# Ring depths of a weight pipeline: three raw buffers, four high and four low parts

## What is computed

```python
proj = rms_norm(h, norm1_gain) @ w_in            # 2048 x 2048 and more
q = (xt @ w_q)                                   # peer_w_q
a = einsum('cd,ced->ce', xc, expert_u[ic])       # peer_u: 2048 x 16384
w = gc * gelu(a)
y = einsum('ce,ced->cd', w, expert_v[ic])        # peer_v: 16384 x 2048
u = square(relu(h @ w_up)); x = x + rms_norm(u @ w_down)
```

## Time and profile before

| | before |
|---|---|
| median of 3 runs | 3338.53 us (3335.76 to 3339.82) |
| profiled execution | 3337.88 us, span 3335.7 us |
| mean granted TensorE clock | 0.989 |
| TensorE busy | 3250.5 us, 97% |
| VectorE busy | 2020.4 us, 61% |
| ScalarE busy | 1490.8 us, 45% |
| DMA of the SyncE queue | 598.71 MB, 57.6% of 16 engines |
| low parts L1981 | 1101 times, mean 1223 ns |
| high parts L1760 | 1101 times, mean 1058 ns |

### The profile page before, as it was taken

One profiled execution on the slowest core, in us unless ns is written; L12 is line 12 of the kernel. 1 busy time (PEld: TensorE's weight loads), 2 busy tenths in 40 slices (PEclk: granted clock), 3 DMA queues, 4 the chain that ended last, 5 costly groups with the idle time before them and its releaser, 6 DMA issues.

```text
span 3335.7 us, 38691 instructions
## 1 busy us (share of the span) xinstructions
PE 3250.5 (97%) x15278; PEld 2704.2 (81%) x15278; DVE 2020.4 (61%) x2922; ACT 1490.8 (45%) x1876; POOL 539.9 (16%) x321
## 2 busy tenths in 40 slices
PE   8888999999999999999999999999999999999998
PEld 7677898788888888888888888888888788888886
DVE  6755568884444456666666665565465655555556
ACT  5434444444444444444444444445444544444443
POOL 0100004787778700000000000000000000000000
PEclk9889999999999999999999999999999999999999
DMA  6553456888888877777776665555666566666664
GB/s 207 179 206 95 145 174 189 200 206 207 209 213 205 208 275 247 244 246 245 241 243 217 183 198 183 158 176 172 189 189 199 176 188 189 189 189 189 189 189 151
DMA packets 215092, 658.71 MB, mean 197 GB/s; under 512 B 56128, under 2 KB 56272, under 8 KB 212352
## 3 DMA queue, kind: packets, MB, share of 16 engines
q1 hardware_dynamic: 165680, 598.71, 57.6%
q0 software_dynamic: 49232, 57.54, 7.7%
HBM read 620.38 MB, written 35.78 MB: 197 GB/s over the span
## 4 chain that ended last, share of the span: by engine, by line
PE 88%; DVE 8%; ACT 3%; issue 1%; DMA 0%; DVEq 0%; ACTq 0%; SPq 0%
PE bank L1554 86%; PE bank L1616 2%; DVE wlo L1981 2%; ACT whi L1760 1%; ACT M L1802 1%; DVE AL L2027 0%; DVE M L2267 0%; DVE M L2273 0%; DVE R L2459 0%; ACT M L1750 0%; DVE M L2271 0%; DVE M L2269 0%; DVE M L2084 0%; DVE TMP L2050 0%; DVE M L2284 0%
## 5 line engine op out<-in xcount | busy, mean ns | idle before, releaser
L1981 DVE TENSOR_TENSOR wlo<-raw,whi 128x1024 fp32r<-128x1024 f32 x1101 | 1343.8, 1223 | 1082.1 <-ACT whi L1760 1077.7
L1760 ACT ACTIVATE whi<-raw 128x1024 fp32r<-128x1024 f32 x1101 | 1159.8, 1058 | 1301.5 <-PE bank L1554 1265.0
L1554 PE MATMUL bank<-whi,BH 128*128 128x512 f32 x2344 | 932.5, 398 | 12.8 <-DVE wlo L1981 7.7
L1554 PE MATMUL bank<-whi,BL 128*128 128x512 f32 x2344 | 915.3, 390 | 0.0
L1554 PE MATMUL bank<-wlo,BH 128*128 128x512 f32 x2344 | 913.8, 390 | 0.0
L1554 PE MATMUL bank<-whi,AH 128*128 128x512 f32 (+1 forms) x1952 | 772.4, 396 | 22.5 <-DVE AL L2027 15.2
L1554 PE MATMUL bank<-whi,AL 128*128 128x512 f32 (+1 forms) x1952 | 762.6, 391 | 0.0
L1554 PE MATMUL bank<-wlo,AH 128*128 128x512 f32 (+1 forms) x1952 | 762.0, 390 | 0.0
L2524 POOL DMA_INDIRECT scr_g<-M x256 | 495.0, 1934 | 437.3 <-issue 396.5
L1554 PEld LDWEIGHTS bank<-whi,BH 128*128 128x128 f32 x2344 | 440.9, 188 | 106.2 <-DVE wlo L1981 12.4
L1554 PEld LDWEIGHTS bank<-whi,BL 128*128 128x128 f32 x2344 | 440.5, 188 | 94.3
(11 more groups left out here) (240 smaller groups left out, 1600.6 us busy)
## 6 DMA issues: line engine op xcount, KB each, us to landing
raw<-in_peer_u SPq DMA_DIRECT2D x256, 512.0 KB
raw<-in_peer_v SPq DMA_DIRECT2D x256, 512.0 KB
raw<-in_w_in SPq DMA_DIRECT2D x160, 512.0 KB
raw<-in_w_up SPq DMA_DIRECT2D x128, 512.0 KB
raw<-in_w_down SPq DMA_DIRECT2D x128, 512.0 KB
raw<-in_w_out SPq DMA_DIRECT2D x64, 512.0 KB
raw<-in_w_in_a SPq DMA_DIRECT2D x32, 512.0 KB
scr_g<-M POOLq DMA_DIRECT2D x8, 2048.0 KB, 29.8
```

The lines of the kernel that those rows point to most:

```text
L1554: return e.matmul(outp, l, r, start=start, stop=stop)
L1760: e.activation(whi[:, n % NH, :], raw[:, n % NR, :], ACT.Copy).then_inc(s_hi, 1)
L1981: e.tensor_tensor(wlo[:, n % NH, :], raw[:, n % NR, :], bf(whi[:, n % NH, :]), ALU.subtract).then_inc(s_lo, 1)
```

## The change

The raw ring goes from five slots to three, the rings of high and low parts from three slots each to four. The sum is 3 + 4 + 4 = 11 slots as before. At the start, a raw piece is issued beside a chunk of `x` only for the slots that exist, so three instead of four. Everything else follows from the two constants.

```diff
-    NR, NH, NST = 5, 3, 1080
+    NR, NH, NST = 3, 4, 1080
...
             for j in range(4):
                 go("load_x", j)
                 t_x.append(landing(f"x_landed{j}"))
-                go("load_piece", n_load[0])
-                n_load[0] += 1
+                if j < NR:
+                    go("load_piece", n_load[0])
+                    n_load[0] += 1
```

## The result

In five runs of each kernel on one chip the changed kernel took 3353.38 us (3347.53 to 3354.96) and the kernel before 3336.25 us: ratio 1.0045, 95% interval 1.0034 to 1.0056. The profiled execution took 3353.47 us.

A forecast was written before the change was run, and what follows sets the result against it. TensorE was taken as the bound, busy 3250.5 of 3335.7 us. Terms -9.6 + 1.2 + 0 = -8.4 us against the profiled 3337.9 gave 3329.5; with 0.65 for the median, 3330.2 us, range 3325 to 3346.

The forecast's parts named there:

- starved in the bursts: Rival at the `peer_v` fetches: three raw buffers turn too slowly, 1 to 3 us a burst, 3344 to 3374 us; chance 0.15.
- Term 1: TensorE's waits for low parts that come too late: the deeper ring saves 9.6 us, between 0 and 13.2.
- The twelve waits: TensorE's waits for low parts between 500 and 760 us, during VectorE's routing work: all taken as saved, 7.8 us.
- The early two: TensorE's waits at 118.61 and 138.39 us: gain lost to later VectorE waits, taken at 0, other end 3.6 us.
- Term 3: The start, with three raw pieces issued in the first rush, not five: cost 0, other end 2.5 us.
- Term 2: Raw pieces landing later with three slots: single bursts cost TensorE 0, the double first fetch 1.2 us, between 0 and 4.
- The rule of the Trainium skill: DMA engines alternate between queues by packet, so weight loads land early and bursts cost nothing: 1.2 us less than the sum.

The follow-up runs named there:

- pair of cut kernels: Kernels after and before, each with scratch fetches for chunks 2 to 15 cut to an eighth: 3323.66 us (0.9963) and 3336.73 us (1.0000).
- four of each: Kernel after with four raw, four high and four low slots, room taken from small statistics: 3324.81 us, ratio 0.9961 to the kernel before.
- the multiplications moved: Kernel after with the 128 gate multiplications of `peer_v` on GpSimd in place of VectorE: 3322.95 us, ratio 0.9959 to the kernel before.
- the mended kernels: Kernel after with gate work spread over the chunk (3326.46 us), gate multiplications on GpSimd (3322.95 us), or four raw, high and low slots (3324.81 us).

## Why the prediction was wrong

The forecast was 3330.2 us in 3325 to 3346; 3353.4 is outside, and on the side that had 0.15. It is within the 3344 to 3374 of the rival "starved in the bursts".

**Term 1 (-9.6): right.** The twelve waits between 500 and 760 us are gone: 8.8 us in 500 to 800 us, forecast 7.8. The one at 3317 is gone with its 1.2 us. The early two were taken up at 123 and 149 us as forecast (1.2 and 2.4, measured 1.33 and 2.54). The pair of cut kernels puts the whole at 13.1 us. What the sum left out is small delays in which the weight load is late, not the matmul: the count by starts has 5.8 us from 1100 to 1900 us before, 3.5 with four of each and 1.3 with the multiplications moved. In `peer_v` they come once a chunk, 0.25 us each, right at the end of the gate work (1513.61 in the kernel before): there the lead was already used up before the change.

**Term 3 (0): right.** The delays counted up to 25 us changed from 8.5 to 8.4 us.

**Term 2 (+1.2): wrong, +25.3.** The step that failed is this: "from issue to use there are now 5.8 + 3 x 2.72 = 14.0 us, less 2.35 for the split, so a load may take 11.6 us". At the double fetch, where the term had its 1.2 us, TensorE starts 0.5 us late; nearly all of the 25.3 come behind the single ones, priced at 0. The 9.0 us for a load in the burst were right (8.9). The 14.0 held only for a ring whose lead is full when the burst comes, which the prediction took from ScalarE's waits over the whole span. For the load issued at 1521.84 TensorE was ready at about 1531.4 (its last start 1531.13 and 0.227), 9.5 us later, so the load might take 7.2 us. Of the 4.5 us that lacked, the gate work ahead of the fetch had taken 3.3 or somewhat less; the rest, by subtraction, is lead that the chunk before had not given back. The rows for this stood in reach: VectorE's three low parts at 1512.34 in the earlier trace rows are its catching up behind the gate work, and GpSimd's fetch waits for exactly that work to end, so the burst always comes when the lead is at its lowest. The prediction looked at burst and gate work one at a time. Where either was taken away, the time came to 3328.7 and 3323.7 us, near its 3330.2.

The step behind it failed too: "the fourth goes out only after the first is split ... 8 us to land. So a single burst costs TensorE 0." It priced the burst by itself and had no term for the way back. With three slots a slot turns in a landing of 4.3 and a split of 2.35 us, which would be 2.2 us a piece against TensorE's 2.72; once the burst's own loads have landed, the trace has 2.38, so 0.34 us of lead a piece. By the same sum five slots could turn at 1.3. In the chunk shown 4.0 us came back; drawn were 3.3 by the gate work and 8.9 - 5.8 = 3.1 by the load in the burst. The 2.4 us between are an estimate, and a high one: TensorE starts 1.75 us late there, and 0 to 2.8 us behind the other single fetches from 1294 us on.

**The rival** had the right place and price: from 1250 us on, TensorE starts 0.6 to 2.8 us late behind eleven of thirteen bursts, and it had said 1 to 3. Its point of decision, a load of 11.6 us, rested on the same full lead and was too high, and so its chance was too low. What it had for its mechanism, a ring that turns too slowly, is what the trace shows, drawn out over the whole chunk rather than over the burst's four pieces.

**The rule of the Trainium skill** ("DMA: Bandwidth & Descriptors", DMA queue model, Arbitration), that the queues take turns packet by packet, was expected to make the bursts free. They weren't: 8.9 to 9.9 us for the loads beside the fetch at 1520.62, against a median of 4.3. The starts of the trace's DMA packets tell how far the rule goes here. The fetch's first megabyte is 128 packets of 8 KB, which start from 1521.86 to 1525.08 us; no packet of a weight piece starts in that time, though one piece has been issued at 1521.84, and its first packet starts at 1525.71. From 1525.5 to 1529.5 us the second megabyte and the weight pieces start 192 and 163 packets, of 4 KB each. So turns are taken there, as the page says, but only behind the whole first megabyte. After the first microsecond of the fetch's packets no weight packet starts among those of 8 KB in twelve of the fourteen single fetches. Behind the fetch at 1386.59 the load is issued after 0.4 us instead of 1.2; 73 weight packets start in between, and it took 6.65 us. Why the first megabyte goes ahead as a whole stays open.

**What to look for, checked.** ScalarE waits for raw "some 60 times, 100 us or more": in the expert layer alone it was 187 times and 312 us, with 55 times in `peer_u`, which was not expected and cost TensorE nothing. "TensorE waits for low parts in `peer_v`" had been named as the sign that the forecast is wrong, and it was there. The 4.5 us of waits for low parts forecast for TensorE came true in the mended kernels (4.4 to 6.3).

## What to carry to other kernels

A ring's full depth counts against a disturbance only if the ring is full when it comes. Find what stands ahead of each burst, above all the work whose end releases it, and add up what both take. Then work out the way back: the time of a landing plus the time until the slot is free again, divided by the number of slots, is the ring's time for a piece. What it lacks to the consumer's pace is all the lead that a piece gives back. Before taking room from another ring for depth, try to spread the disturbing work or to give it to an idle engine; here both cost nothing.

## What was not expected of the hardware

TensorE's clock made some of the waits dearer. The stretches at 1252, 1260 and 1264 us after (columns as above; the first number in brackets is TensorE's matmuls):

```profile
1252.00:1260.00 8.00, 5.58 (x25) 4.34 (x24) 1.87 (x3) 1.06 (x1) 0.00 (x0) 1.00 1.01 349
1260.00:1264.00 4.00, 4.00 (x12) 2.94 (x10) 1.23 (x1) 2.12 (x2) 0.00 (x0) 0.57 0.62 218
1264.00:1272.00 8.00, 8.00 (x36) 6.52 (x36) 5.92 (x6) 3.95 (x4) 0.00 (x0) 1.00 0.70 223
```

Behind the wait of 2.42 us at 1259.55 the granted clock is 0.57 from 1260 to 1264 us, matmuls start 0.43 us apart instead of 0.227 (the lower level, 1.2 GHz), and 12 start where the kernel before starts 19. The granted clock also falls to the lower level at two more of the new waits, at 1352 and 1803 us, for 3.4 us each time: some 5 of the 25 us. TensorE had waited 2.42, 2.68 and 2.00 us just before. The wait of 2.17 us at 1623.77 had none behind it, so the length of the wait alone doesn't tell.

A low part on VectorE took 1297 ns in place of 1224 in the stretch from 1480 to 1580 us where GpSimd did the multiplications, 1063 ns each. That is a mean; the median there is 1226 ns, and six of the 37 took 1443 to 1799 ns. It cost no visible time: TensorE is busy 800.00 of 800 us in the stretch from 1100 to 1900 us.
